# Expert results added to the residual by accumulating transfers issued from the Pool queue

## What is computed

```python
    x = x + jnp.concatenate([a_out, b_out], axis=-1) @ w_out
    x = x + hier_moe(rmsnorm(x, g_ffn), w_rg, b_rg, w_re, b_re, w_e_in, w_e_out)
...
    # hier_moe: 32 experts, top 2 per token
    out = out + gates[:, e:e + 1] * (act @ w_e_out[e]).astype(jnp.float32)
...
    y_prompt = rmsnorm(xp, g_final)[:, N_META:]
    y_sample = rmsnorm(xs, g_final)
```

## Time and profile before

| what | us |
|---|---|
| median of 3 runs | 685.34 |
| lowest and highest | 685.03, 685.75 |
| the profiled execution's own time | 683.86 |
| its span, first to last instruction | 682.1 |
| from the end of the last scatter's landing (649.67) to the span's end | 32.4 |

### The profile page before, as it was taken

How to read it: one execution, slowest core, us unless ns; L and a number is a source line. 1 busy time by engine, 2 the same in 40 slices (tenths; PEclk the granted TensorE clock), 3 DMA queues, 4 the chain that set the end, 5 groups by cost and what they waited for, 6 DMA issues and landing times.

```text
span 682.1 us, 8166 instructions
## 1 busy us (share of the span) xinstructions
PE 572.4 (84%) x3099; PEld 356.2 (52%) x3100; DVE 311.9 (46%) x506; ACT 151.0 (22%) x281; POOL 162.8 (24%) x218
## 2 busy tenths in 40 slices
PE   3998998999799999997999888999997978777600
PEld 2447998999577766664455474444332323222200
DVE  2262999999869744554234574121120211111035
ACT  3122211212333345554021110111010001010122
POOL 3051433451133244114000022112120212000125
PEclk9998997999669999997999969999997989898955
DMA  8602522201400600002394359999999999999383
GB/s 279 171 1 61 187 63 61 63 1 46 146 1 1 247 1 1 1 1 74 88 428 187 138 208 371 423 423 424 422 425 425 422 426 423 425 425 426 130 290 132
DMA packets 42168, 144.41 MB, mean 212 GB/s; under 512 B 6902, under 2 KB 23310, under 8 KB 33943
## 3 DMA queue, kind: packets, MB, share of 16 engines
q1 hardware_dynamic: 37527, 134.78, 50.6%
q0 software_dynamic: 4608, 9.18, 3.5%
HBM read 136.16 MB, written 15.39 MB: 222 GB/s over the span
## 4 chain that ended last, share of the span: by engine, by line
PE 50%; DVE 20%; DMA 19%; issue 5%; POOL 2%; ACT 2%; SPq 1%; DVEq 0%; POOLq 0%; ACTq 0%
DMA low<-in_w_expert_in 17%; DVE big L1557 14%; PE ps L1229 11%; PE ps L1079 8%; PE ps L886 4%; PE ps L1254 4%; PE ps L985 3%; PE ps L950 3%; PE ps L1012 2%; PE ps L929 2%; PE ps L998 2%; PE ps L980 2%; PE ps L963 2%; PE ps L983 1%; PE ps L1216 1%
## 5 line engine op out<-in xcount | busy, mean ns | idle before, releaser
L1557 DVE SCALAR_TENSOR_TENSOR big<-low,cwt,big 128x590 f32<-128x590 f32 x120 | 125.2, 1044 | 3.9
L1229 PE MATMUL ps<-big,cw 128*64 128x512 f32 x352 | 81.3, 615 | 13.3 <-DMA big<-in_w_expert_in 10.5
L1864 DVE TENSOR_TENSOR low<-low,ps 128x256 f32<-128x256 f32 x16 | 6.7, 421 | 184.6 <-ACT low L1457 184.6
L929 PE MATMUL ps<-cw_r 128*128 128x288 f32 x256 | 77.5, 303 | 8.3 <-DVE low L1572 5.1
L929 PE MATMUL ps<-low_r,cw_r 128*128 128x288 f32 x256 | 77.1, 301 | 0.0
L929 PE MATMUL ps<-cw_r,big_r 128*128 128x288 f32 x256 | 76.9, 300 | 0.0
L1229 PEld LDWEIGHTS ps<-big,cw 128*64 128x64 f32 x352 | 28.6, 141 | 64.5 <-issue 64.5
L657 POOL TENSOR_TENSOR big_r<-big,cw_r 128x1024 fp32r<-128x1024 f32 x16 | 42.8, 2681 | 65.6 <-ACT cw_r L1338 65.6
L1079 PE MATMUL ps<-cw,low 128*128 128x512 f32 x128 | 56.3, 595 | 0.7 <-DVE low L1677 0.5
L929 PEld LDWEIGHTS ps<-cw_r 128*128 128x128 f32 x256 | 49.9, 195 | 9.4 <-issue 9.4
L929 PEld LDWEIGHTS ps<-cw_r,big_r 128*128 128x128 f32 x256 | 49.8, 194 | 0.0
(11 more groups left out here) (245 smaller groups left out, 847.1 us busy)
## 6 DMA issues: line engine op xcount, KB each, us to landing
big<-in_w_expert_in SPq DMA_DIRECT2D x22, 2048.0 KB, 28.1
big<-in_w_expert_out SPq DMA_DIRECT2D x22, 1024.0 KB, 29.3
low<-in_w_expert_in SPq DMA_DIRECT2D x10, 2048.0 KB, 31.2
big<-in_w_in SPq DMA_DIRECT2D x20, 512.0 KB, 4.8
low<-in_w_expert_out SPq DMA_DIRECT2D x10, 1024.0 KB, 33.0
cw<-in_w_out SPq DMA_DIRECT2D x1, 4096.0 KB, 12.9
big<-y_dram SPq DMA_DIRECT2D x8, 512.0 KB, 7.3
big<-in_cache_k SPq DMA_DIRECT2D x1, 2048.0 KB, 10.9
```

The costliest lines, as they stand in the source:

```text
L929: mm = pe.matmul(ps[:, 2 * (j % 2) + half, 0:HALF], w[:, k, :], h[:, k, cols], start=k == 0 and m == 0, stop=k == KD - 1 and m == 2)
L1229: mm = pe.matmul(ps[TILE * half:TILE * half + TILE, GU_BANK[s], :], xt[s][:, k, TILE * half:TILE * half + TILE], wi[2 * s + half][:, k, :] ...
L1557: link(dve.scalar_tensor_tensor(conv[:, i, :], u[:, i, j:j + CW], cwt[:, i, j:j + 1], conv[:, i, :], ALU.mult, ALU.add))
```

## The change

Nothing ahead of the last stage is altered. In the last stage SP no longer loads `y_dram`, and `experts_done`, `y0` and `y1` are gone. Pool, after `each_further_tile`, issues transfers from `y_dram` straight into `x` with `accum_op=ALU.add`: the transfer reads the DRAM rows and adds them to what is in SBUF. `add_rows(c, 0)` adds the first expert rows of chunk c, `add_rows(c, 1)` the second, and the second waits until the first has landed. Chunk 4 takes two transfers for each. In all that is 12 transfers. ACT now waits for `y_loaded[c]` instead of `sum_ready`. All five norms are made by VectorE (`norm_out`); Pool keeps the roots, and two of them stand between its transfers.

```diff
-POOL_ADDS = (0,)
-POOL_NORMS = (0, 1)
...
-            sp.wait_ge(experts_done, 1)
             for c in range(NC):
-                for k, dst in enumerate((y0[c], y1[c])):
-                    lo = k * COLS + P * c
-                    if c < 4:
-                        sp.dma_start(dst, y_dram[lo:lo + P, :]).then_inc(y_loaded[c], 16)
-                    else:
-                        sp.dma_start(dst[0:16, :], y_dram[lo:lo + 16, :]).then_inc(y_loaded[c], 16)
-                        sp.dma_start(dst[32:64, :], y_dram[lo + 32:lo + 64, :]).then_inc(y_loaded[c], 16)
-            for c in range(NC):
-                if c in POOL_NORMS:
-                    sp.wait_ge(yo2_ready, POOL_NORMS.index(c) + 1)
-                else:
-                    sp.wait_ge(yo_ready, c + 1 - sum(q < c for q in POOL_NORMS))
+                sp.wait_ge(yo_ready, c + 1)
...
             each_further_tile(pool, more, table)
-            pool.sem_inc(experts_done, 1)
-            def scale_out(c):
-
-                pool.wait_ge(scaled, POOL_NORMS.index(c) + 1)
-                pool.wait_ge(gfn_loaded, 16)
-                pool.tensor_tensor(yo[c], yo[c], gfn, ALU.mult).then_inc(yo2_ready, 1)
-
-            for c in range(NC):
-                w = ROWS[c]
-                if c in POOL_ADDS:
-                    pool.wait_ge(y_loaded[c], 32)
-                    pool.tensor_tensor(y0[c][0:w, :], y0[c][0:w, :], y1[c][0:w, :], ALU.add).then_inc(y01_ready, 1)
-                if c >= 1:
-                    root(stat[0:ROWS[c - 1], 39 + c:40 + c])
-                if c - 2 in POOL_NORMS:
-                    scale_out(c - 2)
-            root(stat[0:ROWS[4], 44:45])
+
+            def add_rows(c, k):
+
+                lo = k * COLS + P * c
+                if k == 1:
+                    pool.wait_ge(y_loaded[c], 16 if c < 4 else 32)
+                for r0, r1 in ((0, P),) if c < 4 else ((0, 16), (32, 64)):
+                    pool.dma_start(x[r0:r1, c, :], y_dram[lo + r0:lo + r1, :], accum_op=ALU.add).then_inc(y_loaded[c], 16)
+
+            add_rows(0, 0)
+            add_rows(1, 0)
+            add_rows(2, 0)
+            add_rows(0, 1)
+            add_rows(3, 0)
+            add_rows(1, 1)
+            add_rows(4, 0)
+            add_rows(2, 1)
+            root(stat[0:P, 40:41])
+            add_rows(3, 1)
+            root(stat[0:P, 41:42])
+            add_rows(4, 1)
+            for c in range(2, NC):
+                root(stat[0:ROWS[c], 40 + c:41 + c])
...
             for c in range(NC):
                 w = ROWS[c]
-                act.wait_ge(sum_ready, c + 1)
+                act.wait_ge(y_loaded[c], 32 if c < 4 else 64)
...
-                if c - 1 in POOL_NORMS:
-                    act.wait_ge(rstd_ready, ROOTS_BEFORE + c)
-                    act.activation(yo[c - 1], x[:, c - 1, :], ACT.Copy, scale=stat[:, 39 + c:40 + c]).then_inc(scaled, 1)
...
-            def add_experts(c):
-                w = ROWS[c]
-                if c in POOL_ADDS:
-                    dve.wait_ge(y01_ready, POOL_ADDS.index(c) + 1)
-                else:
-                    dve.wait_ge(y_loaded[c], 32 if c < 4 else 64)
-                    link(dve.tensor_tensor(y0[c][0:w, :], y0[c][0:w, :], y1[c][0:w, :], ALU.add))
-                dve.tensor_tensor(x[0:w, c, :], x[0:w, c, :], y0[c][0:w, :], ALU.add).then_inc(sum_ready, 1)
...
             def norm_out(c):
                 w = ROWS[c]
-                if c in POOL_NORMS:
-                    return
...
-            add_experts(0)
             for c in range(NC):
-                if c + 1 < NC:
-                    add_experts(c + 1)
                 mean_square(c)
                 if c >= 1:
                     norm_out(c - 1)
```

## The result

The changed kernel takes 689.9 us (median of 4 runs, 688.32 to 691.22) against 685.18 (now the median of 4 runs too): a ratio of 1.0071, interval 1.0049 to 1.0093. It is slower, by 4.7 us. The profiled execution took 691.22, its span is 689.4.

What follows compares the result with a forecast made beforehand. TensorE and weights bound the expert stage, untouched; the last stage is its own path. Transfers of 24.5 us complete chunk 4 at 677.1, plus 8.2: 685.3 against 682.1, +3.2, so 688.5 (chance 0.45; +0.8 to +6; wider range 681 to 703).

Steps and rivals of the forecast that it cites:

- The rate: Last stage: the twelve accumulating transfers read 4.59 MB twice and take 24.5 us, between 22.2 and 27.2.
- The start at no cost: Start of the last stage: Pool issues the first transfer at about 650.70, one hop of 0.02 saved, counted as nothing.
- Issues of about 1.0 us, beside the data: Pool's queue: 12 issues need 12.1 to 24.8 us; taken near the low end, at 1.0 to 1.5 each beside the transfers.
- The waits in Pool's queue, covered by 1 us: Pool's last transfers wait for landings and roots, but earlier transfers fill the queue until 675.6; covered by 1 us.
- The norms at no cost: VectorE takes over the norms of chunks 0 and 1, 2.5 us, while it has nothing else to do: nothing.
- The tail: From chunk 4's landing at 677.1 to the end at 685.3: 8.2 us, of which 3.84 for the stores.
- The rival of copy rate: Last stage: accumulating transfers run at a copy's rate, issues and waits rule; −6.1 us, 679.2; chance 0.22.
- The rival of issue pace: Pool's queue: issues of 2.07 us each set the pace; +4.6 us, 689.9; chance 0.12.
- The rival of no overlap: Last stage: successive accumulating transfers do not overlap, 40 us in all; +16.8 us, 702.1 or more; chance 0.21.
- chunk 0 complete late with Pool idle: Last stage: chunk 0 complete after 665 with Pool idle before its waits would show that transfers do not overlap.
- wrong as a whole if anything before 650 moves by more than half a microsecond: Ahead of the last stage: no instruction changed there, so a move above half a microsecond would make the forecast wrong.

Runs made afterwards that it cites:

- e3: The changed kernel with all five roots behind Pool's last transfer; one run, 688.3 us.
- e4: The kernel before with all five norms on VectorE, its loads and additions as they were; 682.17 us, ratio 0.9958.
- e5: The kernel before with all norms and all additions on VectorE, no accumulating transfer; 680.75 us, ratio 0.993.
- e1: The changed kernel with its twelve Pool transfers as plain copies into scratch tiles, the experts' results not added; one run, 682.1 us.
- f2: As e5, but chunk 4 and the second rows of chunk 3 are added by accumulating transfers; 680.81 us, ratio 0.9944.
- h1: As f2, with the roots of chunks 0 and 1 ahead of the last two transfers on Pool's queue; 681.55 us, ratio 0.9937.

## Why the prediction held

It forecast +3.2 us and 688.5; measured are +4.7 and 689.9, of which +4.1 is in the stage. By its own steps, in us from the scatter's landing (predicted from 649.67, measured from 652.85):

| step | predicted | measured |
|---|---|---|
| Pool's first issue | 1.0 | 1.5 |
| chunk 4 complete | 27.4 | 29.3 |
| last norm ends | 31.8 | 33.5 |
| end of the span | 35.6 | 36.6 |

- *The rate* was the term that decided, and it was right. It was taken at 24.5 us for all rows, from the bounds 22.2 and 27.2, because the DMA engines read 1.03 busy with one stream. From the first accumulated packet to the last are 25.7 us in the changed kernel (656.06 to 681.78), and 24.7 in e3, without the roots in between. The engines gave 207 to 211 GB/s for long stretches, with a slower start (176 GB/s) and dips. The mechanism is the predicted one, an engine's time per packet that doubles (328 ns against 159), though the share of 1.03, from which it was argued, is no sure sign of it. The Trainium skill (Collectives: The Full Stack, The bandwidth ceiling: the fold count and why AG ≠ RS ≠ AR) says that a ReduceScatter runs at about half of an AllGather's rate, since each piece needs two source reads on the same ring; the trace agrees with the ratio, with 328 over 159 = 2.06 by packets and 414 over 211 = 1.96 against SP's loads. No run here shows the two reads themselves.
- *The start at no cost* was wrong by half a microsecond: Pool's first transfer starts 1.54 us after the landing (0.64 of it behind Pool's last branch), where SP's first load started after 1.05. The first bytes came 1.7 after the issue, for 1.4.
- *Issues of about 1.0 us, beside the data*: right (median 1.0).
- *The waits in Pool's queue, covered by 1 us*: wrong for the last one. From the first issue to the completion of chunk 4 took 27.7, where 26.4 were predicted; without the roots between (e3) it took 26.7. So of the 1.9 us that chunk 4 is late, about 1 is this wait, half a microsecond the start, and the rest the data.
- *The norms at no cost*: right, and more was in it than the working said. It did not price the removal of Pool's products by itself. Measured alone it is −3.0; with it, and +7.1 for the transfers, each of the two terms is much larger than what they leave together.
- *The tail* after chunk 4 was taken as 8.2 and is 7.3. The stores behind the last norm took 689.4 − 686.37 = 3.0 instead of the 3.84 that was to stay. They take 3.0 in e4 and e5 too, which also have no Pool product: before, the stores of chunks 1 and 2 stood until 675.27, when the second product was done, and three stores of a whole chunk were issued in the 3.0 us ahead of the last norm's end. That they delay the last one is likely, not shown apart. This error has the opposite sign to those above: by luck the stage's miss is 0.9 and not 1.9.
- *The rival of copy rate* fell. e1 shows what it would have given, a stage of 30.0, 2.4 less than before and not 6.1, since the copies were slower than SP's and chunk 4 was complete 22.7 us after the landing, where its sum had 18.2. *The rival of issue pace* fell by Pool's idle time and e1; that its 689.9 is the measured median to the digit is chance. *The rival of no overlap* fell: a transfer of 512 KB landed 9.1 us after its issue at the median, and all 8.75 chunks took 25.7, so that about three were under way at a time. Its sign in the prediction, chunk 0 complete late with Pool idle, was badly chosen: chunk 0 came at 665.5 by before's clock, past the 665 named, and that is only the half rate with a slow start.
- *The sign "wrong as a whole if anything before 650 moves by more than half a microsecond"* came true in the first profile, by 3.2 us, and it was drawn too tight: the same landing differs by 3.8 us over the 13 profiles, and by 3.7 between the two of the changed kernel.

## What to carry to other kernels

Price an accumulating transfer as two plain ones in DMA time, also beside others. It can pay only where the DMA engines have idle time and the adding engine has none; here the versions that were built for that (f2, h1) were not told apart from plain additions on VectorE. An in-order queue that mixes transfers which wait for landings with small results that others need passes each wait on to them. When a change has two parts, time each alone: here the one that looked incidental held the gain. And before a stretch that nothing changed is used as a sign, take a second profile of the same kernel.

## What the runs showed of the hardware

A packet of 4,096 B held its DMA engine 159 ns when it was copied, from SP's queue or from Pool's, and 328 ns when it was added. Plain direct transfers from Pool's queue moved 309 to 360 GB/s from 654 to 660 with the engines 0.92 to 1.00 busy, where SP's moved 414. The issue of a plain one held Pool 0.54 us, that of an accumulating one 1.0.

Pool and VectorE got in each other's way in the kernel before. Pool's two products and VectorE beside them:

```profile
664.66 2.34 POOL L846 TENSOR_TENSOR big<-big 128x1024 f32<-128x1024 f32 x1
665.64 2.45 DVE L1901 TENSOR_TENSOR big<-big 128x1024 f32<-128x1024 f32 x1 [1.58 <-DMA big<-y_dram]
670.57 1.22 DVE L1902 TENSOR_TENSOR x<-x,big 64x1024 f32<-64x1024 f32 x1
670.92 4.33 POOL L846 TENSOR_TENSOR big<-big 128x1024 f32<-128x1024 f32 x1
671.78 1.27 DVE L1915 SCALAR_TENSOR_TENSOR big<-x,stat,big 128x1024 f32<-128x1024 f32 x1
```

The first product began alone and took 2.34 us, as Pool's addition did with VectorE idle; VectorE's addition began beside it and took 2.45 instead of 1.22. The second product began beside VectorE's addition and took 4.33, and VectorE's instructions kept their 1.22 and 1.27. So the one that began later lost, 1.2 us at 1.4 us of overlap (665.64 to 667.00) and 2.0 us at 2.1 (670.92 to 673.05), as if it stood still meanwhile. That this is the reason why removing the products gained 3.0 us is likely, but was not measured apart.
